# Stick-breaking heads: the running sum's PSUM bank also receives products with key differences, and the exponential reads it there; three projection tiles loaded in the last stage

## The reference

```python
z = jnp.einsum('bhqd,bhkd->bhqk', qb, kb) * scale
mask = s_idx[None, :] < t_idx[:, None]
log_beta = jax.nn.log_sigmoid(z)
log_1m = jnp.where(mask, log_beta - z, 0.0)
log_a = log_beta + lax.cumsum(log_1m, axis=3, reverse=True) - log_1m
A = jnp.where(mask, jnp.exp(log_a), 0.0)
outs.append(jnp.einsum('bhqk,bhkd->bhqd', A, vb))
```

## Time and profile before

| what | value |
| --- | --- |
| median of 3 runs | 1552.05 us |
| lowest and highest | 1549.65 and 1554.65 us |
| the profiled execution's own time | 1554.16 us |
| its span in the profile | 1552.4 us |
| PE busy | 1468.7 us, 95% |
| DVE busy | 1049.3 us, 68% |
| ACT busy | 805.4 us, 52% |
| POOL busy | 300.2 us, 19% |
| mixing stage | about 360 to 780 us of the span |

### The profile page before, as it was taken

How to read it: one execution, slowest core, us unless ns; L and a number is a source line. 1 busy time by engine, 2 the same in 40 slices (tenths; PEclk the granted TensorE clock), 3 DMA queues, 4 the chain that set the end, 5 groups by cost and what they waited for, 6 DMA issues and landing times. The chain is left out here.

```text
span 1552.4 us, 36775 instructions
## 1 busy us (share of the span) xinstructions
PE 1468.7 (95%) x15392; PEld 1243.9 (80%) x15392; DVE 1049.3 (68%) x1522; ACT 805.4 (52%) x1396; POOL 300.2 (19%) x307
## 2 busy tenths in 40 slices
PE   6999999995998999999889996999999999999998
PEld 6999999995777777777658875878888888888886
DVE  6244436445878887789766769998888665544555
ACT  6254445344777877778665543333333343433452
POOL 6233425340001011010100004543333000100000
PEclk9999999997999999999999998999999999999999
DMA  4433562646613224121244567798777585675553
GB/s 183 143 125 126 184 233 75 233 124 196 145 34 85 54 51 106 40 51 42 80 96 122 144 222 239 271 306 280 265 250 247 193 305 190 231 271 192 194 183 136
DMA packets 120220, 258.06 MB, mean 166 GB/s; under 512 B 9200, under 2 KB 50288, under 8 KB 119808
## 3 DMA queue, kind: packets, MB, share of 16 engines
q1 hardware_dynamic: 115536, 239.33, 47.4%
q10 hardware_dynamic: 3744, 13.85, 2.2%
q0 software_dynamic: 784, 2.65, 0.7%
HBM read 167.67 MB, written 86.85 MB: 164 GB/s over the span
## 5 line engine op out<-in xcount | busy, mean ns | idle before, releaser
L2415 DVE TENSOR_TENSOR tail_tl<-tail_down_raw,tail_th 128x1024 fp32r<-128x1024 f32 x84 | 102.0, 1256 | 96.2 <-ACT tail_th L2097 96.2
L2097 ACT ACTIVATE tail_th<-tail_down_raw 128x1024 fp32r<-128x1024 f32 x84 | 84.4, 1052 | 129.1 <-PE tail_bank L2701 114.5
L2701 PE MATMUL tail_bank<-tail_th 128*128 128x512 f32 x336 | 131.0, 390 | 0.0
L2701 PE MATMUL tail_bank<-tail_th,tail_tl 128*128 128x512 f32 x336 | 131.0, 390 | 0.0
L2701 PE MATMUL tail_bank<-tail_tl,tail_th 128*128 128x512 f32 x336 | 130.7, 389 | 0.0
L689 PE MATMUL inproj_acc<-xn_xl,inproj_wh 128*128 128x348 f32 (+1 forms) x384 | 123.4, 321 | 0.0
L689 PE MATMUL inproj_acc<-xn_xh,inproj_wl 128*128 128x348 f32 (+1 forms) x384 | 123.2, 321 | 0.0
L689 PE MATMUL inproj_acc<-xn_xh,inproj_wh 128*128 128x348 f32 (+1 forms) x384 | 123.2, 321 | 0.0
L569 DVE TENSOR_TENSOR inproj_wl<-xn_raw,inproj_wh 128x1024 fp32r<-128x1024 f32 x27 | 34.8, 1287 | 94.5 <-ACT inproj_wh L445 94.5
L2631 PE MATMUL tail_bank<-tail_th,tail_ah 128*128 128x512 f32 x240 | 93.8, 391 | 3.2 <-ACT tail_p L2194 1.2
L2631 PE MATMUL tail_bank<-all_mh,tail_ah 128*128 128x512 f32 x212 | 84.9, 400 | 10.5 <-DVE tail_al L2320 10.5
(11 more groups left out here) (388 smaller groups left out, 4411.9 us busy)
## 6 DMA issues: line engine op xcount, KB each, us to landing
tail_down_raw<-u_scratch SPq DMA_DIRECT2D x56, 512.0 KB, 3.5
tail_raw<-in_w_up SPq DMA_DIRECT2D x32, 512.0 KB, 6.6
tail_w_quad<-in_w_down SPq DMA_DIRECT2D x16, 1024.0 KB, 8.9
d_scratch<-tail_w_quad SPq DMA_DIRECT2D x16, 1024.0 KB, 8.4
u_scratch<-tail_u_sums SPq DMA_DIRECT2D x16, 1024.0 KB, 5.9
tail_down_raw<-d_scratch SPq DMA_DIRECT2D x32, 512.0 KB, 4.4
xn_raw<-in_w_in SPq DMA_DIRECT2D x27, 512.0 KB, 5.0
p_scratch<-inproj_out ACTq DMA_DIRECT2D x26, 520.0 KB, 2.7
```

Of the source, the lines that this page charges most:

```text
L2097: act.activation(op_high[b][:, j, :], down_raw[c % len(down_raw)][:, j, :], ACT.Copy).then_inc(down_high, 1)
L2415: dve.tensor_tensor(op_low[b][:, j, :], down_raw[c % len(down_raw)][:, j, :], op_high[b][:, j, :].bitcast(F32), ALU.subtract).then_inc(dow ...
L2701: last = pe.matmul(downs[pass_of(c) % 2][o][:, :], u[:, own_tile], w[:, f * HALF:(f + 1) * HALF], start=(n == 0 and f == 0 and j == 0), st ...
```

## The change

The bank `cb` now gets the exponent itself. `tri` and `rest` hold -1 where they held 1, so the softplus sums are subtracted. For the first key block of a group PE adds the scores (keys `ks` times `qh` and `ql`) to the bank; for each further block b it adds the product with the key difference k[b] - k[b+1], which turns the scores of the block before into those of block b. The difference is held in the new tile `kd`, split into a high and a low half like `ks`. The factor 1/8 moves into the split of the queries. DVE's L1331 goes, ACT's exponential reads the bank, and `rest` waits for that exponential (`weights`) and no longer for DVE. The differences are made by DVE in place in `k2` (`set_kd`), split by ACT (`high_kd`) and DVE (`low_kd`). The memory for `kd` and `k_edge` comes from the three weight tiles, which are now loaded at the start of the tail, behind `vec` and on one semaphore with it. `osum(2)` moves behind `project_first`.

```diff
+def kd_part(p):
+    return slice(K_EDGE, KEYS - P) if p == 0 else slice(0, K_EDGE)
...
-            split_at[free_before(i, p) + 1] = (i, p)
+            split_at[free_before(i, p) + 5] = (i, p)
+    kd_at = {1: (0, 0)}
+    for now, part in split_at.items():
+        kd_at[now + 3] = part
...
+                sp.wait_ge(kd_low, split_no(i - 1, p) + 1)
                 start.load_part(sp, i, p, start.qk_loaded[p])
...
-                if n == 2:
-                    for k in range(W_EARLY):
-                        sp.dma_start(w_raw[:, k, :], w_out[k]).then_inc(w_loaded, 16)
...
+            for s in range(2):
+                pool.wait_ge(stored[s], 16 * (IN_TILES // 2))
             for t in (tri, rest):
-                pool.memset(t[:, :], 1.0).then_inc(zeroed, 1)
+                pool.memset(t[:, :], -1.0).then_inc(zeroed, 1)
...
-                act.activation(qh[:, :, q_part(p)], q2[:, :, q_part(p)], ACT.Copy).then_inc(qk_high, 1)
+                act.activation(qh[:, :, q_part(p)], q2[:, :, q_part(p)], ACT.Copy, scale=HD ** -0.5).then_inc(qk_high, 1)
...
+            def high_kd(i, p):
+                act.wait_ge(kd_set, 3 * i + 1 + 2 * p)
+                act.activation(kd[:, :, kd_part(p)], k2[:, :, kd_part(p)], ACT.Copy).then_inc(kd_high, 1)
...
-                        part = a[t % 4][:, at(t).off:]
-                        exponent.wait(act, t)
-                        act.activation(part, part, ACT.Exp).then_inc(weights.sem, 1)
+                        off = at(t).off
+                        tri_done.wait(act, t)
+                        pv_done.wait(act, t - 4)
+                        act.activation(a[t % 4][:, off:], cbs[at(t).h][:, off:], ACT.Exp).then_inc(weights.sem, 1)
...
+            def set_kd(i, p):
+                dve.wait_ge(qk_low, 2 * split_no(i, p) + 2)
+                cols = kd_part(p)
+                if p == 0:
+                    last = dve.tensor_tensor(k2[:, :, cols], k2[:, :, cols], k2[:, :, cols.start + P:], ALU.subtract)
+                else:
...
+            def low_kd(i, p):
+                dve.wait_ge(kd_high, split_no(i, p) + 1)
+                low = kd[HD:P, :, kd_part(p)]
+                dve.tensor_tensor(low, k2[HD:P, :, kd_part(p)], low.bitcast(F32), ALU.subtract).then_inc(kd_low, 1)
...
-                    t = now - 4
-                    if is_task(t):
-                        off = at(t).off
-                        tri_done.wait(dve, t)
-                        pv_done.wait(dve, t - 4)
-                        dve.tensor_tensor(a[t % 4][:, off:], z[t % 5][:, off:], cbs[at(t).h][:, off:], ALU.subtract).then_inc(exponent.sem, 1)
+                    if now - 3 in split_at:
+                        set_kd(*split_at[now - 3])
+                    if now - 1 in kd_at:
+                        low_kd(*kd_at[now - 1])
...
+                        left = (ks if first else kd)[:, h, b * P:(b + 1) * P]
+                        for x in (qh, ql):
+                            pe.matmul(cbs[h][:, :], left, x[:, h, g * SBW:(g + 1) * SBW], start=(first and x is qh), stop=False,
+                                      skip_group_check=True)
                         soft_low.wait(pe, t)
-                        if at(t).first:
-                            exponent.wait(pe, t - 2)
-                        sums(tri, tri_r, t, at(t).first).then_inc(tri_done.sem, 1)
+                        sums(tri, tri_r, t, False).then_inc(tri_done.sem, 1)
...
-                        exponent.wait(pe, t)
+                        weights.wait(pe, t)
                         sums(rest, rest_r, t, False).then_inc(rest_done.sem, 1)
...
-            sp.dma_start(vec[:, :, :], vecs).then_inc(vec_loaded, 16)
+            sp.dma_start(vec[:, :, :], vecs).then_inc(first_loaded, 16)
+            for k in range(W_EARLY):
+                sp.dma_start(w_tile(k), w_out[k]).then_inc(first_loaded, 16)
...
-            dve.wait_ge(vec_loaded, 16)
+            dve.wait_ge(first_loaded, FIRST_LOADS)
             scale_o(0)
...
                         mean(2)
-                        osum(2)
...
             project_first()
+            osum(2)
             var(2)
```

More of the change, by code:

```diff
@@ L778 @@
 W_EARLY = 3
+FIRST_LOADS = (W_EARLY + 1) * 16
 LAP_SLOTS = 8
@@ L935, in stage_mix @@
         for p in range(PARTS):
-            split_at[free_before(i, p) + 1] = (i, p)
+            split_at[free_before(i, p) + 5] = (i, p)
+    kd_at = {1: (0, 0)}
+    for now, part in split_at.items():
+        kd_at[now + 3] = part
+    kd_first = {}
+    for t in task_ticks:
+        x = ticks[t]
+        if not x.first:
+            kd_first.setdefault((x.i, 0 if x.b * P >= K_EDGE else 1), t)
     lower_part = [min(t for t in of_group[i, 1] if ticks[t].b * P < K_EDGE) for i in range(PAIRS)]
@@ L1074, in _ @@
                 for e, source in enumerate((gate_dram, bonus_dram)):
-                    tile = w_raw[here, W_EARLY, e * (D // 2):(e + 1) * (D // 2)].rearrange("p (q n) -> p q n", q=PAIRS)
+                    tile = w_raw[here, 0, e * (D // 2):(e + 1) * (D // 2)].rearrange("p (q n) -> p q n", q=PAIRS)
                     sp.dma_start(tile, source[:, there, 0:P].rearrange("q p n -> p q n")).then_inc(w_loaded, 16)
@@ L1194, in sticks @@
                         z_done.wait(act, t)
-                        exponent.wait(act, t - 5)
-                        act.activation(z[t % 5][:, off:], zb[:, off:], ACT.Copy, scale=HD ** -0.5).then_inc(z_copied.sem, 1)
+                        soft.wait(act, t - 5)
+                        act.activation(z[t % 5][:, off:], zb[:, off:], ACT.Copy).then_inc(z_copied.sem, 1)
                     if is_turn(t):
@@ L1221, in sticks @@
                         high_k(*split_at[now - 1])
+                    if now in kd_at:
+                        high_kd(*kd_at[now])
                     yield
@@ L1509, in sticks @@
                     if is_task(t):
+                        i, h, g, b, first = at(t).i, at(t).h, at(t).g, at(t).b, at(t).first
+                        if first:
+                            weights.wait(pe, t - 2)
+                        for part in range(PARTS):
+                            if kd_first.get((i, part)) == t:
+                                pe.wait_ge(kd_low, split_no(i, part) + 1)
+                        left = (ks if first else kd)[:, h, b * P:(b + 1) * P]
+                        for x in (qh, ql):
+                            pe.matmul(cbs[h][:, :], left, x[:, h, g * SBW:(g + 1) * SBW], start=(first and x is qh), stop=False,
+                                      skip_group_check=True)
                         soft_low.wait(pe, t)
-                        if at(t).first:
-                            exponent.wait(pe, t - 2)
-                        sums(tri, tri_r, t, at(t).first).then_inc(tri_done.sem, 1)
+                        sums(tri, tri_r, t, False).then_inc(tri_done.sem, 1)
                     yield
@@ L1714, in stage_tail @@
         HALF_M = 4 * KD * HALF
-        first_gate, first_bonus = (w_raw[:, W_EARLY, e * HALF:(e + 1) * HALF].rearrange("p (q n) -> p q n", q=PAIRS) for e in range(2))
+        first_gate, first_bonus = (w_raw[:, 0, e * HALF:(e + 1) * HALF].rearrange("p (q n) -> p q n", q=PAIRS) for e in range(2))
         dev, rsd, ors = (over(name, [P, PAIRS, QT], mh_at + 2 * HALF_M - (n + 1) * ROW) for n, name in enumerate(("dev", "rsd", "ors")))
```

38 lines of the change are left out of this document (27 added, 11 removed).

## The result

The changed kernel takes 1614.15 us (median of 4 runs, 1611.49 to 1615.26) against 1552.43 us of the kernel before (4 runs): a ratio of 1.0384, with a 95% interval of 1.0361 to 1.0407 (the plain quotient of the medians, 1.0398, lies within it). The forecast was 1604 us, with a range of 1574 to 1630. Direction and size hold. The sum does not hold term by term, as the experiments show.

The account below looks back on a forecast made before the run. The prediction took PE to set the pace of the mixing stage. Its terms, 51.5 - 8 + 5 + 3 + 3 - 2 = 52.5 us, gave 1604.5 us against the median, rounded to 1604, with a range of 1574 to 1630 us.

Parts of the forecast that it names:

- signs: Mixing stage about 470 us, PE busy 95% or more; wrong if under 440, products under 40 or `rest` waits over 15.
- products on PE, less PE's waits given back: Mixing stage: 224 products at 0.23 us add 51.5 us; 8 us of PE's waits for DVE and ACT go.
- `rest` waits for the exponential: Mixing stage: `rest` now waits for ACT's exponential instead of DVE's exponent; 5 us taken, between nothing and 55 us.
- splits of the differences: Mixing stage: eight splits put pieces of 0.9 to 1.6 us on DVE and ACT; 3 us taken, 10 at worst.
- start of the tail: DVE's scaling waits for three weight tiles and `osum(2)` comes later; tail 3 us late, bounds 0 and 6.
- clock in the mixing stage: A term of the sum for the clock in the mixing stage, taking off 2 us.
- Rival 3: Mixing stage: ACT's lag makes every `rest` late by half the upper bound, 27 us on top; about 1630 us, chance 0.13.
- That PE sets it and DVE doesn't: Mixing stage: PE, busy 94%, sets the pace; DVE at 83% keeps up with it and doesn't hold it back.
- Rival 1: Mixing stage: DVE sets the pace and the products fit into PE's gaps; 1539 us, faster, chance 0.06.
- I take all 51.5 as added: Mixing stage: the new products find little PE waiting time to fill, so their whole 51.5 us counts as added.
- rival 2: Mixing stage: new products partly cover PE's hidden breaks and idle time, some 30 of 51.5 us vanish; 1577 us, chance 0.13.
- ACT is mostly through and waits for the scores: Mixing stage: the reason why `rest` waiting for ACT's exponential costs nothing from below; 5 us taken.

## Why the prediction was right

The forecast was right in direction, within its range, and 10 us below the measured time. Its signs held too: the stage is 470.1 us long (470 expected), PE is busy for 95.7% of its middle, DVE for 67% and ACT for 70%, ACT's wait for the scores has grown to 49.3 us, the new products take 52.4 us of PE net, over the 40, and `rest` waits 11.3 us, under the 15 that would have made it wrong. Its sum was right for partly the wrong reasons: the terms that were too high and those that were too low made up for each other, and that is luck. Each term beside what taking it out of the changed kernel, or putting it alone into the kernel before, showed:

| term | forecast | measured |
| --- | --- | --- |
| products on PE, less PE's waits given back | 51.5 - 8 = 43.5 | 28 taken out; 25 put in alone |
| `rest` waits for the exponential | 5 | 11 by moving it; 24.5 put in alone |
| splits of the differences | 3 | 12 taken out |
| start of the tail | 3 | 7.6 put in alone; 5.6 in the changed kernel's trace |
| clock in the mixing stage | -2 | nothing came back: at 0.50 for 18.8 us before, 22.7 after |

28 + 11 + 12 + 7.6 = 59, against a ratio of 1.0384, 59.6 us. That the four add up so well is partly luck, as the wait and the products overlap. No run shows the 2 us that the sum takes off for the clock. What the trace of the kernel before shows is a granted clock of 0.50 for 6.8 of the 345 us of the main stretch (3.4 from 477.8 and 3.4 from 600.7), which makes its 0.99; in the changed kernel's whole stage it was 0.50 for 3.9 us longer than before. Rival 3's sum adds 25 for its 27 and doesn't take off the 5 that the forecast already holds.

**What sets the pace.** That PE sets it and DVE doesn't, the step on which all rested, holds. Without the products and with the exponential moved, DVE is busy for 74% of the main stretch and not 83%, and the ratio is 1.0131; take off the tail's 0.0049 and the splits' 0.0080, each measured in another kernel, and 1.000 is left, give or take some 6 us by the three intervals. DVE's 63 us were worth nothing that can be measured. What isn't excluded is a gain of a few us that the clock took back, as it is at its lower level for 33.3 us of that kernel's stage, where the traces of the stage as it was have 13.6 to 27.9. Rival 1's 1539 us falls all the same. It had the shares for it, 75% for weight loads and 83% for DVE, yet relieving DVE gave nothing measurable, and doubling the score products on PE cost 25 us: with weight loads at 79% of the stretch (273.22 of 345) PE had 5.8 us of idle time left.

**The step that failed on the products** is "I take all 51.5 as added" with 8 given back. PE's own time for them was right (52.4 us net), and so was the argument against rival 2, that the break only moves ahead. The range of what could be given back (0 to 21.3) was right too, but the upper end was nearer to the truth: 17.0 us of idle time in the kernel before. I gave back only the waits with a name; of the 10.7 us of "issue" the doubled products left 4.0. Idle time without a named cause is room as well.

**The step that failed on the wait** is "ACT is mostly through and waits for the scores". The earlier trace rows say that of 34 of the 95 score copies in that stretch; at the others ACT came when the scores were there or nearly so. The wait falls due in each tick, so the ticks in which ACT comes late decide. Half the upper bound, as in rival 3, would have been nearer for the kernel before; in the changed one the wait is smaller because PE has more to do in each tick (19.8 us without products, 14.9 with one, 12.1 with both).

**The splits** were mis-sized: 12 us against 3. My upper bound counted one stop of PE per split; each brings two pieces on DVE and one on ACT. That this is why they cost more wasn't shown.

**The tail** was 2.5 us late at DVE's first scaling, the number of the forecast, but 5.6 in the profile. Two parts are not in the sum: the lower clock behind the late scaling (1.5 us) and the new gap at `osum(2)`. That gap cost 1.4 up to the split projection, and less than 1 behind it.

## What to carry to other kernels

Before work moves off an engine, take one semaphore of the change alone into the old kernel: here a single later release cost as much as 224 products (24.5 and 25 us). Price new work on the pacing engine by its pitch (the distance from one start to the next, here 0.23 us where the records last 0.40 and 0.48), and count as room all of that engine's idle time, named or not (17.0 of 28.8 us were filled here); and look at what a reader in the same memory bank now holds back (here `rest`, by 11.3 us). In a pipeline whose order is fixed, place the step that another engine waits for as early as its inputs allow, not where its predecessor stood (11 us here). When a trace shows a slow stretch at a gap, as here the 6.8 us at a granted clock of 0.50, look for the one that it replaces before you count it as a loss.

## What the runs showed that I had not expected

The same two products per task that take 51.5 us of PE's time cost 25 to 28 in two quite different kernels, and not for the same reason. Put in, they filled 17.0 us of PE's idle time. Taken out, they left 14.6 us of new idle time and 17.5 us more of the stage at a granted clock of 0.50, and PE's other work took 10.9 us longer. And the slow stretch went with the gap: with only `osum(2)` moved, the 6.8 us at 0.50 moved from `osum(2)` (from 798.6) to `var(2)` (from 809.0), and each stretch begins inside the gap there, of 3.3 us and of 6.2.
